# Router query weights in transfers of 120 and 8 rows, and block 0's power one unit later, in a two-layer encoder trunk

## What is computed

```python
def peer(xn, wq, k1, k2, u, v):
    q = (xn @ wq).reshape(B, S, PEER_HEADS, 2, PEER_HALF)          # 8 heads, 2 halves of 128
    s1 = jnp.einsum('bshd,nd->bshn', q[..., 0, :], k1)
    s2 = jnp.einsum('bshd,nd->bshn', q[..., 1, :], k2)
    t1, i1 = lax.top_k(s1, PEER_TOPK)                              # top 16 of 128, each side
    t2, i2 = lax.top_k(s2, PEER_TOPK)
    ...                                                            # top 16 of the 256 pairs: idx, top_s
    gate = jax.nn.softmax(top_s, axis=-1)
    def block(args):                                               # 128 tokens at a time
        x_blk, i_blk, g_blk = args
        act = jax.nn.gelu(jnp.einsum('td,ted->te', x_blk, u[i_blk]))
        return jnp.einsum('te,ted->td', (g_blk * act).astype(v.dtype), v[i_blk])
```

## Time and profile before

| what | value |
|---|---|
| median of 3 runs | 3384.79 us |
| lowest and highest | 3380.03 and 3387.12 us |
| the profiled execution: its time | 3379.86 us |
| the profiled execution: its span | 3377.7 us |
| PE, DVE, POOL busy | 85%, 63%, 20% of the span |
| gathers: 512 of 2 MB | 1073.77 MB of 1229.54 MB moved |
| mean traffic over the span | 364 GB/s |

### The profile page before, as it was taken

How to read it: one execution, slowest core, us unless ns; L and a number is a source line. 1 busy time by engine, 2 the same in 40 slices (tenths; PEclk the granted TensorE clock), 3 DMA queues, 4 the chain that set the end, 5 groups by cost and what they waited for, 6 DMA issues and landing times.

```text
span 3377.7 us, 26696 instructions
## 1 busy us (share of the span) xinstructions
PE 2857.0 (85%) x8488; PEld 1554.9 (46%) x8488; DVE 2121.9 (63%) x4777; ACT 655.3 (19%) x1509; POOL 664.4 (20%) x563
## 2 busy tenths in 40 slices
PE   6999999888897777777779999888889777777777
PEld 5877864444443333333338786444444332332332
DVE  4454556666666666666666755666666666666665
ACT  3344411111111111111114531111111111111111
POOL 0000022222222222222210002222222222222221
PEclk9999999999999999999999999999999999999999
DMA  6544579999999989999995347999999999999997
GB/s 212 169 162 149 185 327 427 425 428 426 426 427 427 426 372 427 427 427 427 427 389 183 125 151 314 428 427 426 427 426 427 427 424 428 423 415 428 419 421 331
DMA packets 138471, 1229.54 MB, mean 364 GB/s; under 512 B 12896, under 2 KB 13664, under 8 KB 67552
## 3 DMA queue, kind: packets, MB, share of 16 engines
q0 software_dynamic: 73728, 1073.77, 75.1%
q1 hardware_dynamic: 63888, 148.67, 12.6%
q10 hardware_dynamic: 720, 5.44, 0.4%
HBM read 1225.74 MB, written 2.10 MB: 364 GB/s over the span
## 4 chain that ended last, share of the span: by engine, by line
PE 45%; DMA 41%; DVE 9%; ACT 2%; issue 2%; POOL 0%; SPq 0%; DVEq 0%; POOLq 0%; ACTq 0%
DMA ring_sb<-in_peer_uv_dram,idx_cur 39%; PE bank L1145 21%; PE bank L879 15%; PE bank L929 6%; DVE ring_sb L1618 5%; PE bank L941 1%; ACT diag L705 1%; ACT shared L702 1%; PE bank L1093 0%; ACT w_parts L376 0%; DVE shared L1627 0%; DVE shared L1623 0%; DVE shared L1621 0%; DMA ring_sb<-in_mlstm_w_out_dram 0%; DVE w_parts L382 0%
## 5 line engine op out<-in xcount | busy, mean ns | idle before, releaser
L1145 PE MATMUL bank<-ring_sb,diag 128*128 128x512 f32 x4096 | 1936.3, 624 | 466.0 <-ACT diag L705 465.8
L1618 DVE CUSTOM_DVE_ANT_0 ring_sb<-ring_sb,arena 128x2048 f32<-128x2048 f32 x512 | 1173.5, 2292 | 673.2 <-DMA ring_sb<-in_peer_uv_dram,idx_cur 670.2
L1145 PEld LDWEIGHTS bank<-ring_sb,diag 128*128 128x128 f32 x4096 | 784.2, 198 | 1577.4 <-issue 842.3
L520 POOL DMA_INDIRECT ring_sb<-in_peer_uv_dram,idx_cur x512 | 634.5, 1239 | 1921.8 <-PE bank L1145 1887.2
L879 PE MATMUL bank<-w_parts,actT_hi 128*128 128x512 f32 x1664 | 521.0, 395 | 13.6 <-DVE w_parts L382 9.1
L702 ACT ACTIVATE shared<-shared 128x1 f32<-128x1 f32 x512 | 103.8, 203 | 2029.2 <-DVE shared L1623 2029.2
L382 DVE TENSOR_TENSOR w_parts<-ring_sb,w_parts 128x2048 fp32r<-128x2048 f32 x100 | 228.3, 2290 | 209.2 <-ACT w_parts L376 209.2
L879 PEld LDWEIGHTS bank<-w_parts,actT_hi 128*128 128x128 f32 x1664 | 311.5, 189 | 80.8 <-issue 14.5
L879 PE MATMUL bank<-w_parts,actT_lo 128*128 128x512 f32 x832 | 325.8, 392 | 0.0
L376 ACT CAST w_parts<-ring_sb 128x2048 fp32r<-128x2048 f32 x100 | 190.7, 1909 | 302.2 <-DMA ring_sb<-in_mlstm_w_in_dram 159.2
L705 ACT ACTIVATE diag<-const,shared 128x128 f32<-128x128 f32 x512 | 205.6, 402 | 155.0 <-DVE shared L1627 154.4
(11 more groups left out here) (166 smaller groups left out, 1007.6 us busy)
## 6 DMA issues: line engine op xcount, KB each, us to landing
ring_sb<-in_mlstm_w_in_dram SPq DMA_DIRECT2D x48, 1024.0 KB, 5.2
arena<-in_peer_wq_dram SPq DMA_DIRECT2D x28, 1024.0 KB, 12.6
ring_sb<-in_attn_w_in_dram SPq DMA_DIRECT2D x20, 1024.0 KB, 5.2
ring_sb<-in_mlstm_w_out_dram SPq DMA_DIRECT2D x16, 1024.0 KB, 5.1
ring_sb<-in_attn_w_out_dram SPq DMA_DIRECT2D x16, 1024.0 KB, 5.1
ring_sb<-in_peer_uv_dram,idx_cur POOLq DMA_INDIRECT x512, 21.7
ring_sb<-in_peer_wq_dram SPq DMA_DIRECT2D x4, 1024.0 KB, 7.9
arena<-in_attn_w_in_dram SPq DMA_DIRECT2D x4, 1024.0 KB, 9.6
```

The source lines that it names most:

```text
L520: nc.gpsimd.indirect_dma_start(out=uv_slot[at], out_offset=None, in_=uv_rows, in_offset=bass.IndirectOffsetOnAxis(ap=idx_cur[par][:, k:k + ...
L1145: last = mm(acc[n][:, :], diag[slot_of(gu, k)][:, :], v_slot[at][:, n * CH:(n + 1) * CH], start=False, stop=end and k == TOPK - 1, skip_gr ...
L1618: v.tensor_tensor_reduce(u_slot[at], u_slot[at], xn[b], 1.0, 0.0, ALU.mult, ALU.add, dots[:, c]).then_inc(dot_done, 1)
```

## The change

Two edits. First, each half of a head's `wq` is loaded by two transfers in place of one: rows 0 to 119 and rows 120 to 127, into the same place. Every transfer adds 16 to the semaphore, so both waits of PE are for counts twice as high. Secondly, POOL does the power of norm 2, block 0, in front of gather 2 of unit 10 in place of unit 9; DVE still computes the mean square in unit 9.

```diff
                 def load(h, slots=wq_slot, landed=wq_landed):
                     for i in range(2):
-                        sp.dma_start(slots[i].rearrange("p k n -> p (k n)"),
-                                     rows[bass.ds(h * P + l * HEADS * P, P), i * SLOT:(i + 1) * SLOT]).then_inc(landed[i], 16)
+                        dst = slots[i].rearrange("p k n -> p (k n)")
+                        for r, n in ((0, 120), (120, 8)):
+                            sp.dma_start(dst[r:r + n, :], rows[bass.ds(h * P + (l * HEADS * P + r), n),
+                                                               i * SLOT:(i + 1) * SLOT]).then_inc(landed[i], 16)
...
-                        if l == 0 and u == HEADS + 1 and k == 2:
+                        if l == 0 and u == HEADS + 2 and k == 2:
                             norm(2, [0])
...
-                        pe.wait_ge(wq_landed[half], h * 16 + l * (HEADS - 1) * 16)
+                        pe.wait_ge(wq_landed[half], h * 32 + l * (HEADS - 1) * 32)
...
-                    pe.wait_ge(wq0_landed[c // 2], 16 * (l + 1))
+                    pe.wait_ge(wq0_landed[c // 2], 32 * (l + 1))
```

## The result

The changed kernel takes 3515.09 us (median of 4 runs), the kernel before 3385.03 us beside it (4 runs): a ratio of 1.0396, 95% interval 1.0383 to 1.0408. That is 130 us slower, where a gain of 21 was forecast, and above the upper end of the range (3440). The profiled execution's span is 3511.1 us against 3377.7.

The account below looks back on a forecast made before the run. The prediction took the DMA engines, with one lagging, to bound the PEER stages: −13 −13 (lag relieved in two layers) +7.3 (extra rows) −2.5 (stall) = −21, from 3384.8 to 3364 us; range 3355 to 3440.

Parts of the forecast that it names:

- The bound and the lagging engine: PEER stages: DMA engines alone set the pace, gathers 4.89 us apart; one engine lags the other 15 by some 8 us.
- The count of 16 late steps in layer 1: Between 2368.87 and 3332.51, 16 gathers come 5.8 to 5.9 us after the one before, making 15.5 us.
- The power: Layer 0, POOL: moving it before gather 162 removes the stall after gather 145, −2.5 us.
- SP, the semaphores, more transfers: SP queue: one added instruction on each of 32 loads, issues priced at nothing because SP waits for PE between heads.
- The spread over 15 and 8 engines: wq loads: 120 rows go over 15 engines by 8 each, 8 rows over 8 engines by one.
- If the one left out is the one that lags: PEER stages: the engine without wq rows stops lagging, the others set the time; −13 us in each layer.
- the first rival: The lagging engine keeps its rows: −2.5 us, or +5 if among the eight; within little or no change, chance 0.19.
- The row's cost of 0.306 us on whichever engine: wq loads beside gathers: an 8 KB row takes one engine 0.306 us; 12 heads add +7.3 us on eight engines.
- the second rival: Rows meet in SBUF and slow wq and gathers: +30 to +90 us, 3415 to 3475, chance 0.36 including fewer-engine split.
- the slack: PEER stages: the fast engines' lead of 26 us, taken off the second rival's cost of +59 to +118.
- the upper bound: Second rival, per head loaded beside gathers: half speed for all of the wq and gather mix takes 9.8 us more.

Follow-up runs that it names:

- copies within HBM: Kernel before plus HBM scratch copies of 120, 8, 4, 3, 2, 1 rows behind 12 wq loads: 3408.92, 3408.51, 3410.93, 3387.89, 3390.74, 3383.00 us.
- columns run: Changed kernel, but each wq half cut across columns into two transfers of 128 rows by 4 KB: 3379.84 us, ratio 0.9992.
- 112 and 16: Changed kernel with wq transfers of 112 and 16 rows in place of 120 and 8: 3474.02 us, ratio 1.0270.
- 64 and 64: Changed kernel with wq transfers of 64 and 64 rows in place of 120 and 8: 3487.39 us, ratio 1.0311.

## Why the prediction was wrong, point by point

**The bound and the lagging engine: right.** The PEER stages are set by the DMA engines, and one of them lags. The copies within HBM confirm both: 29 us laid on that engine cost 29 us, laid on three others they cost 6. The count of 16 late steps in layer 1 can't be read exactly: the timeline has ten of 5.6 to 6.0 us by themselves, and the stretch's 191 gathers take 18 us more than plain ones and two `wq` loads would. Nothing hangs on it.

**The power: right in kind.** It was priced at 2.5 us of stall; alone it gave 4.2, with an interval of 0.7 to 6.8 that holds the forecast.

**SP, the semaphores, more transfers: right, at nothing.** The columns run has them all and loses nothing.

**The spread over 15 and 8 engines: right** by the packet counts. The Trainium skill's rule for it (page "DMA: Bandwidth & Descriptors", section "Why a DMA increments its semaphore by 16 and not by 1") holds here: 23 semaphore packets a load in place of 16.

**"If the one left out is the one that lags": this step failed.** The one that lags is reached by transfers of 4, 8 and 120 rows, so it wasn't left out. By the numbering of the same page of the Trainium skill, lowest first, it is engine 3; engine 15 was left out. No run shows an engine's number. The forecast had taken the end of the row to be likelier than the middle, for which no row spoke. The remark of the Trainium skill (same page, section "Latency and other measured facts") that engines 7 and 15 are usually the slower ones doesn't fit this case either, by that numbering. Even if nothing else had happened, the change would have come out at +5, as the first rival had it.

**The row's cost of 0.306 us on whichever engine: this step failed and decided the case.** It was measured where each engine writes to its own partitions. In transfers of 120 and 8 rows the same rows take the rate down by some four tenths: 220 in place of 386 GB/s alone, 263 in place of 427 beside gathers, with the share full in both; and a gather's row, which the change doesn't touch, goes from 0.62 to 1.01 us. This was the second rival, at 0.36. The time lies outside its range as well (3515 against 3475), and the term that was mis-sized is mainly the slack: from 59 to 118 us gross it took off 26, the lead that the fast engines have over the slow one. The likely reason, argued and not measured by itself, is that the slow engine keeps its rows and is held up like the rest, so there is no slack to take off; it still works alone for 10 us at the end. Measured are 128 us for 12 heads, 10.7 each where the upper bound had 9.8, and 9.5 for heads 0 and 1, which the prediction had priced at nothing because they are loaded ahead of the gathers: there PE waits for them.

That the partitions' place in SBUF is what the engines share is shown by elimination and by size: it isn't the number of engines alone (112 and 16), nor of transfers (columns), and copies of 120 rows that leave SBUF alone cost no more than their rows. No trace shows which engine writes which partition. So why 120 and 8 rows lose more than 64 and 64, and those more than 112 and 16, stays open; that 15 and 8 engines are fewer than 16 may be a part of it.

## What to carry to other kernels

A busy share of 1.0 says nothing about the rate: read GB/s beside it, and when a transfer's shape is changed, its rate alone is worth a look first. Rows dealt to other DMA engines still go to the same partitions of SBUF; a tensor of 128 partitions is best loaded by transfers of all 128, and if it must be cut, by columns. And an engine that lags has to be found before it is relieved: small copies of 2, 3, 4 and 8 rows that touch nothing else find it in a few runs. A copy of one row doesn't serve: the packet counts show it spread over all 16. Count the packets before such a run is read.

## What the runs showed of the hardware

- Transfers of less than 128 partitions into a tile of 128 run at 220 to 275 GB/s with all engines busy, one of 128 at 386 in the same window; beside gathers they hold those up too (263 in place of 427 GB/s for 29 us, and 1.01 in place of 0.62 us for a gathered row of 16 KB on its engine). A copy of 120 rows into HBM beside gathers does not (427).
- The same bytes cut by columns, 4 KB a row, cost nothing that could be measured (0.9982 to 1.0002).
- Copies from HBM to HBM of 8 KB rows cost a busy engine about what a load does: 28 to 29 us for 96 rows, 0.29 to 0.31 us each.
- A copy of 2, 3, 4 or 8 rows uses that many engines; a copy of a single row of 8 KB uses all 16, in pieces of 512 B.
- 2.4 MB more on three engines cost 6 us of 3381, and 3.1 MB on four cost 29: one engine of 16 carries the kernel's time.
